# MLP products of a two-layer fp32 backbone in 2x2x2 blocks, by seven block products in place of eight

## The reference

```python
def squared_relu_mlp(h, w1, w2):
    return jnp.square(jax.nn.relu(h @ w1)) @ w2      # 1024 -> 4096 -> 1024

mod = s_c @ w_mod[l] + b_mod[l]                      # 6 x 1024 per layer, for latent and for context
x = x + ga1 * y
x = x + ga2 * squared_relu_mlp(rms_norm(x, p['g_norm2']) * (1.0 + sc2) + sh2, p['w_mlp1'], p['w_mlp2'])
```

## Time and profile before

| | us |
|---|---|
| median of 3 runs | 2021.47 (2019.67 to 2023.76) |
| profiled execution | 2017.82 |
| its span | 2016.0 |
| TensorE busy | 1845.9 (92%) |
| DVE busy | 1081.2 (54%) |
| ACT busy | 700.9 (35%) |
| POOL busy | 529.6 (26%) |

### The profile page before, as it was taken

How to read it: one execution, slowest core, us unless ns; L and a number is a source line. 1 busy time by engine, 2 the same in 40 slices (tenths; PEclk the granted TensorE clock), 3 DMA queues, 4 the chain that set the end, 5 groups by cost and what they waited for, 6 DMA issues and landing times.

```text
span 2016.0 us, 28541 instructions
## 1 busy us (share of the span) xinstructions
PE 1845.9 (92%) x11692; PEld 1543.3 (77%) x11692; DVE 1081.2 (54%) x1719; ACT 700.9 (35%) x941; POOL 529.6 (26%) x156
## 2 busy tenths in 40 slices
PE   5899998879877999999999979999788979999998
PEld 3788896568766888888888868878567758787776
DVE  3384836567337766857757854853566652222122
ACT  4433257543205212212212236234763353222230
POOL 0224512000211221222222222362200324434342
PEclk8899999999987999999999999999899989999999
DMA  8421112000131223332323223111200012222221
GB/s 324 173 105 43 64 42 105 1 1 1 63 125 63 106 104 127 118 113 100 112 103 125 105 92 125 64 63 43 105 1 1 32 60 97 85 103 83 104 84 63
DMA packets 23906, 172.84 MB, mean 86 GB/s; under 512 B 2628, under 2 KB 3050, under 8 KB 4842
## 3 DMA queue, kind: packets, MB, share of 16 engines
q1 hardware_dynamic: 23786, 171.09, 23.0%
HBM read 162.69 MB, written 8.39 MB: 85 GB/s over the span
## 4 chain that ended last, share of the span: by engine, by line
PE 73%; issue 7%; DVE 7%; ACT 7%; DMA 2%; POOL 2%; SPq 1%; DVEq 0%; POOLq 0%; ACTq 0%
PE ps L1720 46%; PE ps L1892 7%; PE ps L1707 5%; POOL w_lo L471 1%; PE ps L1974 1%; DMA raw<-w_big 1%; PE ps L1690 1%; PE ps L1825 1%; DMA raw<-w_modl 1%; PE ps L2020 1%; DVE mx L1396 1%; ACT tmp L638 1%; PE ps L2027 1%; PE ps L2052 1%; PE ps L2055 1%
## 5 line engine op out<-in xcount | busy, mean ns | idle before, releaser
L471 POOL TENSOR_TENSOR w_lo<-raw,w_hi 128x2048 fp32r<-128x2048 f32 x96 | 445.0, 4636 | 1155.0 <-ACT w_hi L581 1155.0
L581 ACT ACTIVATE w_hi<-raw 128x2048 fp32r<-128x2048 f32 x96 | 183.1, 1908 | 394.2 <-PE ps L1720 356.6
L1720 PE MATMUL ps<-h_hi,w_hi 128*128 128x512 f32 x880 | 265.9, 361 | 0.1
L1720 PE MATMUL ps<-h_lo,w_hi 128*128 128x512 f32 x880 | 260.9, 356 | 0.0
L1720 PE MATMUL ps<-h_hi,w_lo 128*128 128x512 f32 x880 | 260.8, 355 | 0.0
L1050 DVE SCALAR_TENSOR_TENSOR mod_acc<-raw,cs,mod_acc 128x256 f32<-128x256 f32 x392 | 251.2, 709 | 0.0
L1720 PE MATMUL ps<-hid_hi,w_hi 128*128 128x512 f32 (+1 forms) x768 | 234.3, 359 | 0.0
L1720 PE MATMUL ps<-hid_lo,w_hi 128*128 128x512 f32 (+1 forms) x768 | 232.9, 357 | 0.0
L1720 PE MATMUL ps<-hid_hi,w_lo 128*128 128x512 f32 (+1 forms) x768 | 232.9, 357 | 0.0
L1538 DVE SCALAR_TENSOR_TENSOR xT<-ps,modall,xT 128x512 f32<-128x512 f32 x120 | 75.4, 657 | 285.2 <-PE ps L1720 280.4
L1564 DVE TENSOR_TENSOR tmp<-tmp 128x768 f32<-128x768 f32 (+1 forms) x64 | 67.0, 1049 | 193.0 <-ACT tmp L914 192.6
(11 more groups left out here) (298 smaller groups left out, 3080.7 us busy)
## 6 DMA issues: line engine op xcount, KB each, us to landing
raw<-w_big SPq DMA_DIRECT2D x96, 1024.0 KB, 4.8
raw<-w_modl SPq DMA_DIRECT2D x40, 1024.0 KB, 4.8
first_mod<-w_modl SPq DMA_DIRECT2D x8, 1024.0 KB, 19.2
x_keep<-xT SPq DMA_DIRECT2D x2, 3072.0 KB, 10.9
xT<-x_keep SPq DMA_DIRECT2D x2, 3072.0 KB, 10.5
xin<-x_in SPq DMA_DIRECT2D x4, 512.0 KB, 7.9
out<-xout SPq DMA_DIRECT2D x4, 512.0 KB, 2.7
xin<-ctx_in SPq DMA_DIRECT2D x2, 512.0 KB, 9.9
```

The costliest lines, as they stand in the source:

```text
L471: nc.gpsimd.tensor_tensor(w_lo[r][:], raw[raw_r][:], w_hi[r][:].bitcast(F32), ALU.subtract).then_inc(sem("lo_ready"), 1)
L581: nc.scalar.activation(w_hi[w % 2][:], raw[raw_of(w)][:], ACT.Copy).then_inc(sem("hi_ready"), 1)
L1720: ins = mm(pair(g, a, b - a), w[:, k, m * P:(m + 1) * P], mov[hl][:, k, a:b], start=(k == 0 and q == 0), stop=(k == KD - 1 and q == 2))
```

## The change

Both products of a quarter, `h @ w1` and `hid @ w2`, are 1024 x 1024 with 768 or 512 tokens. Each is cut in 2x2x2 blocks (512 inputs, 512 outputs, half the tokens, h = 384 or 256) and formed by the seven products of the Winograd form of Strassen's method. With a11..a22 the halves of the activations and w11..w22 those of the weights (`_blocks` stores them as 1 MB blocks), the seven are, in the order of the phases p = 0..6:

- p0: w11 by a(0,0); p1: w12 by a(1,0); p2: S1 by T1; p3: S2 by T2; p4: S3 by T3; p5: S4 by a(1,1); p6: w22 by T4
- weight sums on DVE, in two chunks of 128x1024 each: S3 = w11 - w21 (`s3`), S1 = w21 + w22 (`s1`), S2 = w22 - S3 and S4 = w12 - S2 (`s2_s4`)
- activation sums on DVE, one instruction of 128 x 4h each: T1..T4 (`t_sum`)

a(i,j) is feature half i and token half j. A quarter has 14 phases P_, 0 to 6 for w1 and 7 to 13 for w2 (a half of 7 phases is called a part below). Every phase is one product of 4 output tiles x 4 k x 3 passes = 48 matmuls of h columns, in two chunks c_ of 24. PSUM banks 0 to 3 and 4 to 7 accumulate across phases; where a sum goes on in the same banks, it is copied out first (`past_sums` on ACT, `evict` on DVE). For each phase:

- ACT: `high_w` of two chunks 128x1024, `high_a` of 128 x 4h, and in the first part `past_sums`
- POOL: `w_lo` of two chunks of 128x1024, in place of one of 128x2048 for each slot
- DVE: `low_a` of 128 x 4h (both inputs in SBUF), the sums above and `evict`

DVE's order within a part, from the loop over P_ (for a quarter after the first):

```diff
+                for P_ in range(PHASES):
+                    part, p = P_ // 7, P_ % 7
+                    if P_ >= 1:
+                        evict(P_ - 1, 1)
+                    modulation_out(P_)
+                    if p == 0:
+                        t_sum(part, 1)
+                        if part or not first:
+                            low_a(l, n_t, P_ + 1)
+                        s3(part, 0)
+                        s3(part, 1)
+                        s1(part, 0)
+                    elif p == 1:
+                        s1(part, 1)
+                        t_sum(part, 2)
+                        low_a(l, n_t, P_ + 1)
+                        low_a(l, n_t, P_ + 2)
+                        s2_s4(part, 0)
+                    elif p == 2:
+                        s2_s4(part, 1)
+                        t_sum(part, 3)
+                        low_a(l, n_t, P_ + 2)
+                    elif p == 4:
+                        t_sum(part, 4)
+                        low_a(l, n_t, P_ + 2)
+                    elif p == 3 or P_ == 5:
+                        low_a(l, n_t, P_ + 2)
+                    elif P_ == 13 and not last:
+                        low_a(l, n_t, P_ + 1)
...
+                    modulation(P_)
+                    evict(P_, 0)
```

POOL and TensorE in the MLP:

```diff
+            def mlp_lows():
+                for P_ in range(PHASES):
+                    p = P_ % 7
+                    for c_ in range(2):
+                        gp.wait_ge(sem("mw_hi"), his.at(2 * P_ + c_ + 1))
+                        if p == 3:
+                            gp.wait_ge(sem("mw_sum"), sums.at(8 * (P_ // 7) + (6, 8)[c_]))
+                        lo = chunk(w_lo[P_ % 2], c_)
...
+                        nc.gpsimd.tensor_tensor(lo, src, chunk(w_hi[P_ % 2], c_).bitcast(F32),
+                                                ALU.subtract).then_inc(sem("mw_lo"), 1)
...
+            def product(P_, n_t):
...
+                for c_ in range(2):
+                    pe.wait_ge(sem("mw_lo"), wlo.at(2 * P_ + c_ + 1))
...
+                    elif P_ in (2, 6, 8):
+                        pe.wait_ge(sem("hid_ev"), hev.at({2: 0, 6: 2, 8: 4}[P_] + c_ + 1))
...
+                    elif P_ in (9, 11, 13):
+                        pe.wait_ge(sem("x_done"), xd.at({9: 2, 11: 6, 13: 8}[P_] + c_ + 1))
...
+                        pe.wait_ge(sem("op_lo"), oplo.at(4 + P_))
+                        for g in (2 * c_, 2 * c_ + 1):
+                            for k in range(4):
+                                ins = term(g, k)
+                    ins.then_inc(sem("big_done"), 1)
```

The modulation slots are dealt out anew:

```diff
-MOD_AT = ((0, 0), (1, 0), (2, 0), (2, 1), (3, 0), (3, 1))
-OUT_MODS = len(MOD_AT)
+MOD_AT = ((0, 0), (1, 0), (2, 0), (2, 1), (3, 0), (3, 1), (4, 0))
+IN_MODS = len(MOD_AT)
+OUT_MODS_AFTER = ((1, 2, 3, 4, 5, 6, 7), (1, 4, 7))
+Q_MODS = 4
+MOD_SUMS = {2: (0, 0), 3: (0, 1), 5: (1, 0), 6: (1, 1), 9: (2, 0), 10: (2, 1), 12: (3, 0), 13: (3, 1)}
```

More of the change, by code:

```diff
@@ L439, in _ @@
[L439 to L450, removed]
@@ new lines, in mlp_loads, with mod @@
+                def mlp_loads(l, i, last):
+                    def mod(j):
+                        if l == 0 and isinstance(i, int):
+                            load_mod(mslot(MLP_MODS + Q_MODS * i + j), raw_m)
+                        elif l == 0:
+                            load_mod(w_mod[bass.ds(i * Q_MODS + (MLP_MODS + j), 1)]
+                                     .rearrange("o p (k m) -> p (o k) m", k=KD), raw_m)
+                    for part in range(2):
+                        to = (l, i, 1) if part == 0 else (l, i + 1, 0)
+                        more = not (last and part == 1)
+                        if more:
+                            sp.wait_ge(sem("mw_sum"), sums.at(8 * part + 4))
+                            load_block("21", *to)
+                            sp.wait_ge(sem("mw_lo"), los.at(PHASES * part + 10))
+                            load_block("11", *to)
+                        mod(1 + 2 * part)
+                        if more:
+                            sp.wait_ge(sem("mw_lo"), los.at(PHASES * part + 12))
+                            load_block("12", *to)
+                            sp.wait_ge(sem("mw_lo"), los.at(PHASES * part + 14))
+                            load_block("22", *to)
+                            mod(2 + 2 * part)
+                    sums.add(16)
+                    los.add(2 * PHASES)
@@ new lines, in mlp_quarter, with half_sum @@
+            def mlp_quarter(l, n_t):
+                for P_ in range(PHASES):
+                    product(P_, n_t)
+                    for j in MOD_AFTER.get(P_, ()) if l == 0 else ():
+                        mod_slot(P_, j)
+            def half_sum(th):
+                pe.wait_ge(sem("acc_added"), T_("acc").add(4 if th == 1 else 2))
+                all_ones = ones[:, 0:1].to_broadcast([P, P])
+                for a in range(2):
+                    ins = mm(bank(4 + th, 0, HALF), all_ones, sqa[th][:, a, :], start=(a == 0), stop=(a == 1))
+                ins.then_inc(sem("ms_ready"), 1)
```

816 lines of the change are left out of this document (551 added, 265 removed).

## The result

The changed kernel takes 2209.17 us (median, 2206.34 to 2212.26), the kernel before 2022.32 beside it: a ratio of 1.0926, 95% interval 1.0903 to 1.0948. The forecast was 2105 and slower; slower it is, but the time lies above the range's end of 2185. The profiled execution has a span of 2209.6 us.

A forecast was written before the change was run, and what follows sets the result against it. It took POOL's and DVE's mutually exclusive SBUF work, with queue order, to bound the changed MLPs. From 2017.8 us, +23 (layer 0 MLP), +68 (layer 1 MLP), +5 (clock) and -10 (elsewhere) gave 2103.8; predicted 2105, range 2045 to 2185.

The forecast's parts named there:

- TensorE's side: MLP matmuls: 176 ns at 384 columns, 118 at 256; a quarter's fourteen products take 118.3 and 79.1 us.
- The two engines shut each other out: POOL's tensor_tensor and DVE instructions with two SBUF inputs run one after the other; one PSUM input is free of it.
- The sum of the shared work: POOL plus DVE SBUF work in an MLP quarter: 142.9 us in layer 0, 104.8 in layer 1, both above TensorE's.
- The uncovered part of layer 0's quarter: Second-part evictions, near 20 us in layer 0's quarter: 6 us left uncovered by POOL's work, giving a quarter of 149.
- The walk of the first part: Following a quarter's first part by turns: in layer 0 p2 waits 8 to 9 us, the part ends at 72 to 73.
- Outside the quarters: Projections, norms and border outside the MLPs: -10 us together, bounds -35 and +15.
- The border: Between the layers: a table load and a weight copy of 1.9 us leave the path, -4 us.
- Bounds outside the MLPs: Recorded bounds of the sum of terms outside the MLPs: -35 and +15; the range's upper case took +10.
- The output projection of layer 0: Waits for modulation slots there, 13.7 us: one wait stays and one slot is added, -8 us (0 to -13).
- The clock: MLP matmuls after TensorE's long idles run at a lower clock: +5 us in all, bounds 0 and 27.
- Cover holds: Rival in the MLPs: POOL's and DVE's turns stay hidden, TensorE is the bound, 1872 us, 1985 with half the gap; chance 0.08.
- Serial DVE: Rival in the MLPs: POOL covers none of DVE's evictions; quarters of 168 and 120 us, total 2228; chance 0.12.

The follow-up runs named there:

- experiment 1: Changed kernel with POOL's MLP subtractions replaced by memsets that read next to nothing, low halves of the weights zero: 2040.62 us (one run).
- experiment 4: Changed kernel with the MLP weights' low halves made on DVE, none on POOL, and an eviction moved ahead in DVE's queue: 2105.47 us, ratio 1.0399.
- Experiment 6: Changed kernel with layer 1's wait for the copy of x one slot later and slot 1's weight split earlier on ACT: 2208.73 us, ratio 1.0924.
- Experiment 8: Changed kernel with `mod_out` and the new slot's `mod_copy` moved inside the row of scans in both input projections: 2192.36 us, ratio 1.0827.

## Why the prediction was right in sign and short in size

- **TensorE's side** was right. 384 columns take 172 to 176 ns, 256 take 113 to 118; three phases of layer 0 without a wait take 25.4 us, forecast 25.35.
- **The two engines shut each other out**: shown by experiments 1 and 4, and by means of up to 2.89, 2.67 and 1.71 us where 2.34, 1.74 and 1.21 are free. The evictions from PSUM were free of it (128x256 never over 0.485 us), as assumed.
- **The sum of the shared work** was right to 2 us in both layers (142.6 and 106.7, forecast 142.9 and 104.8), and so was layer 1's quarter (109.2, forecast 108) with its long idle ahead of p2 (longest 10.5, forecast 11).
- **The uncovered part of layer 0's quarter** is the step that failed: "6 in layer 0" was 20.9. The evictions that the 6 stood for are 11.7 of it; for the other 9.2, in which DVE has no such work either, the forecast had nothing. By phases, 9.3 are slack where TensorE itself is the bound; 4.7 are evictions in phases 10 and 13, where DVE never stops; the other 6.9 are spread. The walk of the first part came near (76.0, forecast 72 to 73). For the second part (87.6, the forecast's total leaves 76 to 77) nothing was walked: it has the evictions, 384 columns each, and modulation sums in the same queue. Four quarters at 163.5 and not 149 are 58 us, over half of the miss.
- **Outside the quarters** the change costs some 32 us, and the forecast had -10. **The border** was forecast at -4 and is +16.4. The forecast priced the edits that shorten it and not the ones that add to its queues: the modulation sums of the last quarter, which stand ahead of the last residuals, and a wait for the copy of x that stands in the queue ahead of a modulation load. Experiment 6 shows that taking away the second is worth 7 us at the border and nothing clear in the median.
- **Bounds outside the MLPs.** The terms' own bounds add up to -33 and +32, not to the recorded -35 and +15. With +32 for the +10 that the upper end took, it would have been 2212 and not 2190.
- **The output projection of layer 0** gained more than forecast (84 us and not 106: -22, forecast -8), and the input projection lost it: the new slot was priced at its matmuls (1.93 us), and its wait was 7.8 and 10.5 us. Experiment 8 measured both together at 17 (9.3 and 7.2 in the two layers).
- **The clock**: forecast +5 over both MLPs. A quarter has 37 and 32 us at the lower level in layer 0 and 24 in layer 1, against none worth telling before. In layer 0 the term was too small: in phases 0, 2, 7, 9 and 11 of the quarter at 787.51 TensorE is busy from end to end and takes 9.9 to 11.3 us for what takes 8.3 to 8.5 in phases 3, 4, 5 and 12. In the first four of these the shared work fills 8.5 to 11.2 us as well. In phase 11 it fills 5.9, so there the clock binds: 11.2, 11.0, 10.3 and 11.2 us in the four quarters, 10 us in all over 8.4. By the phase sums above, 24 us are the most that it can be in layer 0 (an estimate from one quarter). No run takes it apart from the waits, so its price between these stays open.
- **The rivals.** "Cover holds" is refuted by the means above. "Serial DVE", 168 and 120 a quarter, has the wrong condition for layer 1: POOL runs beside 14.0 of 15.7 us of evictions there. In layer 0 it covers 10.2 of 22.9, so this rival is half true just where the forecast failed, and its 2228 is nearer to the 2209 measured than the forecast's 2105.

## What to carry to other kernels

Add up what two engines exclude each other from as one resource, and do it phase by phase with the larger of that and TensorE's need in each: buffers of two chunks carry little slack from one phase to the next. Add to a long wait of TensorE what the matmuls behind it lose at the lower clock. Work given to an idle POOL is no relief where the pair excludes each other and POOL takes nearly twice as long (2.34 against 1.21 us); given to the busier DVE, it made this kernel nearly 5% faster. Of a small step put into an in-order queue, read what long row it will stand behind: one copy of 0.42 us behind a row of scans cost 7 to 9 us in each layer.

## What was not expected of the hardware

The first modulation sum of a slot, a DVE instruction with one 128x256 input in SBUF and a 128x1 scalar, is shut out too. Its median in the changed kernel is 2.36 us; with no work on POOL (experiment 4) it has one length:

```profile
L1286 DVE TENSOR_SCALAR mod_acc<-raw_m,cs 128x256 f32<-128x256 f32 x32 | 9.7, 346 | 0.0
```

Beside POOL's memsets of 0.95 us (experiment 1) its times are 0.348 at the least, 1.172 in the median:

```profile
L1292 DVE TENSOR_SCALAR mod_acc<-raw_m,cs x32: 348/1172/1240, 651.1 to 1141.2; 128x256 f32<-128x256 f32 x32
L1830 DVE TENSOR_TENSOR op_lo<-hid,op_hi x24: 1224/1481/1760, 674.3 to 2008.6; 128x1536 fp32r<-128x1536 f32 x12, 128x1024 fp32r<-128x1024 f32 x12
```

Each that meets a memset ends some 0.15 us behind the memset's end (784.98 behind 784.83). DVE's `low_a`, with two inputs, is at its two free lengths (1.22 and 1.76) beside the same memsets. So a POOL instruction that reads nothing lets a two-input instruction of DVE pass, but not this one-input form. The Trainium skill, "SBUF — State Buffer", section "Who interferes with whom", states both: two SBUF inputs contend only against a POOL operation that reads SBUF, and a tensor_scalar in a mode that uses two ports contends with any. The trace agrees with the first, and with the second as far as the durations show; which mode ran, no row says. The forecast's rule, two inputs in SBUF, missed this form, of which there are 8 in a quarter of layer 0.
